# Cached keys turned by VectorE, and sample weights regrouped by one product, in a fused decoder step

## What is computed

```python
def dilated_attention_sample(q, k_all, v_all, rel_bias):
    # q: (B,T,H,Dh) are the last T rows of k_all/v_all: (B,L,H,Dh)
    for (w, d) in ((128, 1), (512, 4), (2048, 16)):
        n_k = w // d
        dist = d * jnp.arange(n_k + 1)
        idxs.append(q_idx[:, None] - dist[None, :]); biases.append(pattern_bias(rel_bias, d, n_k))
    ...
    s = einsum('bthc,btkhc->bthk', q, kg) * HEAD_DIM ** -0.5 + bias
    p = softmax(s)
    return einsum('bthk,btkhc->bthc', p, vg)
```

## Time and profile before

| | us |
|---|---|
| median of 3 runs (1082.96 to 1085.27) | 1083.66 |
| the profiled execution, its own time | 1082.67 |
| its span, first to last instruction | 1080.7 |
| PE busy / DVE / ACT / POOL | 1036.0 / 523.0 / 312.7 / 212.4 |
| convolution stage, 280 to 498 us | 218 |

### The profile page before, as it was taken

One profiled execution on the slowest core, in us unless ns is written; L12 is line 12 of the kernel. 1 busy time (PEld: TensorE's weight loads), 2 busy tenths in 40 slices (PEclk: granted clock), 3 DMA queues, 4 the chain that ended last, 5 costly groups with the idle time before them and its releaser, 6 DMA issues.

```text
span 1080.7 us, 15684 instructions
## 1 busy us (share of the span) xinstructions
PE 1036.0 (96%) x5834; PEld 620.1 (57%) x5834; DVE 523.0 (48%) x1175; ACT 312.7 (29%) x665; POOL 212.4 (20%) x240
## 2 busy tenths in 40 slices
PE   7999999999999999999999999989999999889997
PEld 6888875565878777766555554334433333345443
DVE  6836634777733464545556464441111110047674
ACT  2332313777533322301111123111111111244331
POOL 0100001121433352531012111322231110130000
PEclk9999999999999999999999998989999999989999
DMA  9713214940563666663973237989999999974321
GB/s 315 190 31 116 71 50 119 293 101 6 215 213 112 212 211 216 207 244 81 355 270 128 94 105 280 405 340 414 418 410 410 419 420 399 371 288 157 119 78 78
DMA packets 99260, 242.11 MB, mean 224 GB/s; under 512 B 21206, under 2 KB 56958, under 8 KB 84528
## 3 DMA queue, kind: packets, MB, share of 16 engines
q1 hardware_dynamic: 88544, 212.10, 54.1%
q0 software_dynamic: 9920, 26.38, 6.4%
q10 hardware_dynamic: 720, 2.62, 0.6%
HBM read 210.12 MB, written 35.65 MB: 227 GB/s over the span
## 4 chain that ended last, share of the span: by engine, by line
PE 80%; DVE 6%; DMA 6%; SPq 4%; issue 2%; ACT 2%; POOL 0%; POOLq 0%; DVEq 0%; ACTq 0%
PE pair L2921 13%; PE pair L3124 13%; PE pair L2598 10%; PE pair L2976 9%; PE pair L3146 6%; PE pair L3228 5%; PE pair L3223 3%; PE pair L2739 2%; DMA h_dram<-R 2%; DMA R<-in_w_up 2%; PE pair L2713 2%; PE pair L3047 2%; PE pair L2755 2%; PE pair L3111 1%; SPq L707 1%
## 5 line engine op out<-in xcount | busy, mean ns | idle before, releaser
L2921 PE MATMUL pair<-R 128*128 128x264 f32 x672 | 160.2, 389 | 0.2 <-POOL R L1032 0.2
L3124 PE MATMUL pair<-R 128*32 128x512 f32 (+2 forms) x896 | 151.3, 601 | 5.2 <-DMA R<-in_w_up 3.0
L2598 PE MATMUL pair<-R 128*128 128x256 f32 x672 | 149.7, 382 | 0.4 <-DVE R L1755 0.4
L2598 PEld LDWEIGHTS pair<-R 128*128 128x128 f32 x672 | 127.0, 191 | 18.8 <-issue 1.0
L2921 PEld LDWEIGHTS pair<-R 128*128 128x128 f32 x672 | 123.5, 190 | 23.4 <-issue 3.5
L2976 PE MATMUL pair<-R 128*128 128x512 f32 x256 | 116.6, 606 | 0.0
L2329 DVE TENSOR_TENSOR R<-pair,R 128x256 f32<-128x256 f32 x21 | 8.9, 425 | 208.3 <-ACT R L1516 208.3
L3124 PEld LDWEIGHTS pair<-R 128*32 128x32 f32 (+2 forms) x896 | 48.8, 125 | 92.2 <-issue 87.8
L3146 PE MATMUL pair<-R,bias 128*32 128x512 f32 (+2 forms) x448 | 78.0, 611 | 2.7 <-issue 2.1
L2976 PEld LDWEIGHTS pair<-R 128*128 128x128 f32 x256 | 47.7, 192 | 53.3 <-issue 52.6
L3228 PE MATMUL pair<-R 128*128 128x512 f32 x168 | 73.0, 593 | 0.0
(11 more groups left out here) (366 smaller groups left out, 1471.5 us busy)
## 6 DMA issues: line engine op xcount, KB each, us to landing
R<-in_w_gate SPq DMA_DIRECT2D x32, 1024.0 KB, 12.3
R<-in_w_up SPq DMA_DIRECT2D x32, 1024.0 KB, 15.6
R<-in_w_down SPq DMA_DIRECT2D x32, 1024.0 KB, 16.8
R<-in_w_in SPq DMA_DIRECT2D x12, 1024.0 KB, 8.4
R<-in_x_prompt SPq DMA_DIRECT2D x16, 512.0 KB, 3.8
R<-in_cache_k SPq DMA_DIRECT2D x8, 1024.0 KB, 5.0
R<-in_cache_v SPq DMA_DIRECT2D x8, 1024.0 KB, 4.9
R<-y_dram SPq DMA_DIRECT2D x16, 512.0 KB, 5.9
```

The costliest lines, as they stand in the source:

```text
L2598: last = mm(qbank(p, part, k), lhs[:, c, :], rhs[:, c, :], start=(c == 0), stop=(c == 3))
L2921: last = mm(cbank(n, k), lhs[:, c, :], rhs[:, c, :], start=(c == 0), stop=(c == 3))
L3124: last = mm(bk[2 + u][r, :].rearrange("p (w f) -> p w f", w=2), xgT[u][:, c, r], wgu[s][:, :, c, :], start=(c == 0), stop=(c == DC - 1))
```

## The change

Keys are no longer transposed by PE. DVE turns 32x32 blocks of them straight from the ring slot into `kT` (two instructions per part), so each of the sixteen 32-dimension slices of the heads (n = 4j + 2hh + half) has its keys in quarters: partition strip i holds quarter i of the rows. A score is 16 matmuls of 256 columns against a `qbd` in which q is spread over the strips with zeros elsewhere. The softmax goes over two sequences at a time (4 passes in place of 2); since a query's scores now lie in four partitions, minima and sums are combined by small DVE transposes (`by_group`). The weights are moved into place by one product with a permutation matrix (`turn`) and one DVE transpose (`put`). The cache items come in another order, and a key's ring slot is free when DVE has turned it. The `relbd` loads are a quarter as large and come behind two stores of x in SP's queue; the sample's q and k are turned by 32 small matmuls; 16 copies (`q4`) lie in steps 9 to 24 of the prompt attention.

```diff
-ITEMS = [("k", b) for b in range(5)] + [("v", 0), ("k", 5), ("v", 1), ("k", 6), ("v", 2), ("k", 7)] + [("v", b) for b in range(3, NB)]
+ITEMS = [("k", 0), ("k", 1), ("k", 2), ("v", 0), ("k", 3), ("v", 1), ("k", 4), ("v", 2),
+         ("k", 5), ("v", 3), ("k", 6), ("v", 4), ("k", 7), ("v", 5), ("v", 6), ("v", 7)]
...
+def sample_order():
+    parts = []
+    for g in range(NPASS + 1):
+        keys = [[("key", 2 * g + d, gg) for gg in range(NG)] if g < NPASS else [] for d in range(2)]
+        if g == 0:
+            parts += keys[0] + [("score", 0)] + keys[1] + [("score", 1), ("soft", 0)]
+            continue
+        b = 2 * g - 2
+        parts += [*keys[0][0:2], ("norm", g - 1), *keys[0][2:3], ("turn", g - 1), *keys[0][3:4], ("put", g - 1)]
+        if g < NPASS:
+            parts += [("score", 2 * g)]
+        parts += [("weigh", b), *keys[1][0:2], ("sum", b), ("weigh", b + 1), *keys[1][2:4]]
+        if g < NPASS:
+            parts += [("score", 2 * g + 1), ("soft", g)]
+        parts += [("sum", b + 1)]
+    return parts
-ROOM = {"key": 4, "score": 4, "turn": 6, "weigh": 8, "sum": 4}
+ROOM = {"key": 4, "score": 6, "soft": 2, "norm": 2, "turn": 2, "put": 2, "weigh": 8, "sum": 4}
...
@@ SP: relbd, now behind keep_xT(0) and keep_xT(1); the ring
+        for t in range(NT):
+            for hh in range(2):
+                const(relbd[NBUCKET * t:NBUCKET * t + NBUCKET, 16 * hh + t:P:32], I["rel_bias"][:, hh:H:2])
-                    sp.wait_ge(S("kn_full"), 4 * ub + 4)
-                    sp.wait_ge(S("kf_full"), 4 * ub + 4)
+                    sp.wait_ge(S("kt_done"), 4 * ub + 4)
@@ ACT: keep_near, keep_far and keep_ps are gone
+            for s in range(2):
+                act.activation(Es[:, s, :], Es[:, s, :], ACT.Exp, bias=nms[:, s:s + 1], scale=-1.0, accum_out=dens[:, s:s + 1]).then_inc(S("ss_exp"), 1)
@@ DVE, prompt attention
+            if 9 <= n < 25:
+                i, j = divmod(n - 9, 4)
+                dve.tensor_copy(q4[32 * i:32 * i + 32, 4 * j:4 * j + 4, :], qts[32 * j:32 * j + 32, :, :]).then_inc(S("qbd"), 1)
@@ DVE, convolution stage
+        def spread_q(b):
+            dve.tensor_tensor(qbd[b % 2][:, :, 16:32].rearrange("p n (i t) -> p n i t", i=4),
+                              q4[:, :, NT * b:NT * b + NT].unsqueeze(2).broadcast_to([P, 16, 4, NT]),
+                              in_strip.unsqueeze(1).unsqueeze(3).broadcast_to([P, 16, 4, NT]), ALU.mult).then_inc(S("qbd"), 1)
+        def turn_keys(b, gg):
...
+                if b >= 1:
+                    dve.wait_ge(S("ss_done"), b)
...
+            dve.transpose(out[:, 0:4], raw[:, 0:4])
+            dve.transpose(out[:, 4:7], raw[:, 4:7]).then_inc(S("kt_done"), 1)
+        def by_group(cols, op, src, group, out):
+            then(dve.transpose(cols, src))
+            then(dve.tensor_reduce(group, cols.rearrange("p (h i t) -> p h t i", h=2, i=4), AX.X, op))
+            if op == ALU.add:
+                then(dve.reciprocal(group, group))
+            return dve.transpose(out.rearrange("p (h i t) -> p h i t", h=2, i=4),
+                                 group.rearrange("p (h t) -> p h t", h=2).unsqueeze(2).broadcast_to([P, 2, 4, NT]))
...
+            for s in range(2):
+                then(dve.tensor_tensor_reduce(Es[:, s, :], bk[6 + g % 2][:, ROW * s:ROW * s + ROW], bias_s, -1.0, 3e38, ALU.add, ALU.min,
+                                              least[:, s:s + 1]))
+                if 2 * g + s + 1 < NB:
+                    new_bias(2 * g + s + 1)
+            by_group(least_t, ALU.min, least, group_least, nms).then_inc(S("ss_scored"), 1)
...
+        def put_ps(g):
+            dve.wait_ge(S("st_full"), g + 1)
+            if g >= 1:
+                dve.wait_ge(S("so_full"), 2 * g)
+            dve.transpose(PTs.rearrange("p s c x -> p (s c x)"), bk[4]).then_inc(S("st_done"), 1)
@@ PE
+            pe.wait_ge(S("kt_done"), NG * b + NG)
...
+            for hh in range(2):
+                for half in range(2):
+                    for j in range(NG):
+                        n = 4 * j + 2 * hh + half
+                        at = 32 * n + (0 if hh else 16)
+                        last = mm(out[strips[j], ROW * second:ROW * second + ROW], qbd_all[second][:, at:at + 32], kT[:, n, :],
+                                  start=(second == 0 and hh == 0 and half == 0), stop=(second == 1 and hh == 1 and half == 1))
         def turn_ps(g):
+            pe.wait_ge(S("ps_ready"), 2 * g + 2)
...
+            mm(bk[4], regroup, Es.rearrange("p s n -> p (s n)"), start=True, stop=True).then_inc(S("st_full"), 1)
```

More of the change, by code:

```diff
@@ L112, in constants @@
[L112 to L117, removed]
-    r = np.arange(P)
-    c["c_mask"] = (2 * (r[:, None] % 32 // 8) + r[:, None] % 2 == np.arange(AD)[None, :] // DH).astype(np.float32)
-    c["c_sel"] = (r[:, None] % 8 // 2 == np.arange(NT)[None, :]).astype(np.float32)
+    c["c_hot_s"] = hot.reshape(P, SKN).astype(np.float32)
@@ new lines, in constants @@
+    r = np.arange(P)
+    quarter, token = r % 16 // NT, r % NT
+    log = np.full((P, PART + SAMP + NB * SAMP), NEG, np.float32)
+    for i in range(4):
+        log[quarter == i, 0:PART] = log_count(dist[i])[token[quarter == i]]
+    for b in range(NB):
+        own = (np.arange(SAMP)[None, :] // NT == b) & (quarter[:, None] == 0)
+        log[:, PART + SAMP + SAMP * b:PART + 2 * SAMP + SAMP * b] = np.where(own, log_count(new_dist)[token], NEG)
+    c["c_log_s"] = log
+    row_at = 32 * quarter + 8 * (r // 32) + 4 * (r % 32 // 16) + token
@@ L197 @@
[L197 to L206, removed]
@@ L224, with place_of @@
 PARTS_AT = spread_parts()
-def place_of(kind, b, gg=None):
-    return next(s for s, parts in PARTS_AT.items() for part in parts if part[0:2] == (kind, b) and (gg is None or part[2] == gg))
+def place_of(part):
+    return next(s for s, parts in PARTS_AT.items() if part in parts)
 NSTAT = 6
@@ L2096, in sample_part @@
         def sample_part(kind, b, *more):
-            if "norm" in more:
-                normalise_sample(0 if kind == "key" else 1)
+            if kind == "key":
+                turn_keys(b, more[0])
+            if kind == "soft":
+                score_sample(b)
+            if kind == "norm":
+                normalise_sample(b)
+            if kind == "put":
+                put_ps(b)
             if kind == "weigh":
                 mask_sample(b)
-            if "soft" in more:
-                score_sample(b // 4)
-            if kind == "score" and b == 3:
-                spread_q(1)
-                new_bias(1)
             if kind == "sum":
                 keep_sum(b)
-            if "sum" in more:
-                keep_sum(more[-1])
         dve.wait_ge(S("late_in"), 16 * NLATE)
@@ L2867, in weigh_values @@
             for k in range(FARC):
[L2868 to L2869 removed]
+                mm(bk[3][strips[k], :], PTs[:, second, 4 + k, :], KV[slot][:, 4 + k, :], start=False, stop=True)
+            last = mm(bk[3][strips[3], :], PTs[:, second, 7, :], V[:, PT, :], start=False, stop=True)
             last.then_inc(S("so_full"), 1)
@@ L2888, in sample_part @@
         def sample_part(kind, *more):
-            if kind == "key":
-                keys(more[0], more[1])
             if kind == "score":
```

292 lines of the change are left out of this document (127 added, 165 removed).

## The result

The changed kernel takes 1092.95 us in the median of 8 runs (1089.7 to 1098.08), the kernel before 1083.06 us in 8 runs beside it (1080.61 to 1085.88). The ratio is 1.0093 with a 95% interval of 1.0074 to 1.0112: **slower by 9.9 us**, where 4.4 us less was forecast and the range ended at 1089.

What follows compares the result with a forecast made beforehand. PE's busy time was taken to bound the convolution stage. PE work -22.3, new waits for DVE +16.9, head -0.8 and prompt attention +1.8 gave -4.4 us: 1078.3 by the sum, 1079.3 predicted as median, range 1069 to 1089.

Steps and rivals of the forecast that it cites:

- PE's own work: Convolution stage: key parts and weight turns leave PE, scores and permutation products add some; 22.3 us less for PE.
- DVE's prices: Convolution stage: a key part's two transposes cost DVE about 1.2 us; DVE busy about 165 us in all.
- rival with stretched transposes: Convolution stage: beside GpSimd a key part takes DVE 1.75 us, making DVE the bound; 1088 to 1097 us, chance 0.20.
- low end's price: Range's low end, 1069 us: DVE keeps up, with a key part's transposes at 0.8 us, as the weights' scaling runs.
- (a): Stage start: scores 0 and 1 wait for cleared regions, spreads, new keys and eight key parts on DVE; 3.5 us.
- (b): Pass 0, from score 1 in slot 13 to the turn behind slot 19: PE waits 3.6 us for DVE.
- (c): Pass 1, score 4 behind put, while DVE also loads transposed convolution terms: PE waits 2.2 us.
- (d): Pass 2, at the turn and score 6: PE waits 2.1 us for DVE.
- (e): Pass 3: norm and turn share a slot, put and weigh 6 another; PE waits 3.0 and 2.6, together 5.6 us.
- The prompt attention: Prompt attention: 32 small matmuls add 1.1 us, the q4 copies on DVE 0.7; together +1.8 us.
- rival of late weights: Convolution stage: weight loads arrive late in some six groups, so 5 us come back; 1084 us, chance 0.13.
- "slower" rival: Slower outcome, chance 0.22: mainly DVE becoming the bound through stretched transposes (1088 to 1097 us), a little late weights.

Runs made afterwards that it cites:

- gaps filled: Changed kernel with extra PE products, their results overwritten, in four places where PE only waited for DVE; 1087.74 us, ratio 1.0056 to before.
- norm first: Changed kernel with the norm ahead of the next sequence's keys in DVE's list, turns unmoved; 1091.03 us, ratio 1.0083 to before.
- and tail: As norm first, with pass 3's norm, turn, put and first weighing in slots of their own, earlier parts moved up; 1081.31 us, ratio 0.9983 to before.
- less DVE work: Changed kernel without turning each key part's three far pieces from the second sequence on; whole run 2205.99 us, only the 216.6 us stage is read.
- head's loads moved: Changed kernel with the small relbd loads back in their old place, ahead of the two stores of x; 1090.54 us, ratio 1.0070 to before.
- q4 on GpSimd: Changed kernel with the 16 small q4 copies of the prompt attention done by GpSimd, not DVE; 1090.36 us, ratio 1.0060 to before.
- ScalarE's help: As and tail, with ScalarE taking the weights' division and q's spreading for sequences 2 to 7 from DVE; 1076.62 us, ratio 0.9943 to before.
- all of it: As ScalarE's help, plus q4 copies on GpSimd, ScalarE's spreading moved to turn and put, new keys' copies on ScalarE; 1075.23 us, ratio 0.9913 to before.
- before, with gaps: Kernel before the change with only four added PE waits on chained ScalarE instructions in the convolution stage; 1098.93 us, ratio 1.0129 to before.

## Why the prediction was wrong

The whole stage in the ledger, all in us:

| run | length | PE's waits | time at 1.2 GHz | left: work |
|---|---|---|---|---|
| before | 218.2 | 1.1 | 0 | 217.1 |
| after | 227.8 | 20.9 | 20.5 | 196.7 |
| gaps filled | 221.5 | 12.6 | 3.4 | 207.2 |
| norm first | 225.5 | 20.9 | 17.0 | 196.1 |
| and tail | 215.9 | 15.7 | 6.8 | 196.8 |
| less DVE work | 216.6 | 16.5 | 6.8 | 196.7 |
| head's loads moved | 226.2 | 21.3 | 17.1 | 196.4 |
| q4 on GpSimd | 225.6 | 20.2 | 17.1 | 196.8 |
| ScalarE's help | 209.2 | 12.6 | 0 | 196.6 |
| all of it | 209.1 | 10.9 | 3.4 | 196.5 |
| before, with gaps | 232.9 | 10.2 | 10.3 | 217.5 |

The last column is worked out from the others, with half of the low clock. It agrees within 0.7 us over the eight kernels with PE's same work (all but before, gaps filled, and before with gaps), while their low clock runs from 0 to 20.5 us. So the three terms account for the stage to that size.

- **PE's own work: right.** 22.3 us less were forecast, 1.1 of them waits, so 21.2 of work; measured 20.4. One price in it was off: a product among products takes 1.85 us (in the chain of before three in a row take 5.54 at 449.52), not the 1.78 it takes between transposes, so a key part cost PE 0.68 to 0.7:

```profile
449.52 5.54 PE pair L2921 x24
```

  With 0.69 the sum would have been 19.0. The new scores took 1.87 us from their start to the next piece, for 1.88 in the sum. Of the 1.4 that remain 0.7 may be the low clock inside a wait; the rest I didn't split. The 16 in the last line of the earlier trace rows are records, so eight matmuls; the 0.86 each is right.
- **DVE's prices: right.** 1.23 us per key part for 1.2; DVE 157 us busy for 165. The rival with stretched transposes is out by the two rows of the transposes. Its premise is right for the joins with both operands in R, 0.81 beside a working GpSimd for 0.43. The low end's price was taken from the weights' scaling; that scaling runs so fast only while GpSimd idles, 0.61 us for two of 256 elements, and takes 1.26 to 1.50 beside GpSimd.
- **The waits: right place by place, low by 4.0 us.** Against the ledger of the prediction: (a) 4.2 for 3.5 (1.8 at a product, 1.06 and 1.30 at scores 0 and 1), (b) 3.9 for 3.6, (c) 2.9 for 2.2 (0.58 at the turn and 2.31 at score 4), (d) 2.0 for 2.1, (e) 5.8 for 5.6, the rest 2.1 for 1.7. The sum of 18.7 would have been low by 2.2; the 1.8 that I took off for overlapping starts wasn't there.
- **The step that failed: "what the clock does" was missing.** The prediction read in the earlier trace rows that the clock stood at 2.4 GHz nearly throughout and carried that over to a kernel in which PE waits at the turns for 2 to 4 us at a time. Behind three of these places and two more waits (score 4, the first weighing of pass 3) it ran at 1.2 GHz, 20.5 us in all, 10.2 us of cost. The earlier trace rows counts gaps of up to 1.6 us in the prompt attention, and the trace of before has 3.4 us of low clock there, behind two of 1.9 and 1.6 us:

```profile
192.00:194.00 2.00, 1.59 (x8) 1.52 (x8) 1.96 (x8) 0.86 (x4) 0.00 (x0) 0.62 0.93 173
194.00:196.00 2.00, 2.00 (x22) 0.73 (x20) 1.95 (x4) 1.66 (x5) 0.00 (x0) 0.53 1.00 211
```

  That is what could have warned.
- **The prompt attention: +2.3 for +1.8, split wrongly.** The 32 small matmuls take 0.68 us from their start to PE's next piece, for the 0.61 of the earlier trace rows, so 0.1 in place of 1.1. The q4 copies cost 0.7 to 2.0 for 0.7, inside the ends of 0 and 3.3; PE waits there for DVE. What else of the 2.3 there is, is open.
- **The head: 0.8 forecast, about 0.6** as a mean over the profiles, within what single ones move.
- **Weights late, and the rest:** waits for GpSimd 0.8 us in two places; the rival of late weights is out. What lies behind the stage took 580.8 us for 582.4.

Together: -5.4 forecast for the stage, +9.6 measured; the 15.0 between are 10.2 of clock, 4.0 of waits and 0.8 of work. Without the clock's term the kernel would have come out about level with before; without the other two misses it would still have been slower, by some 5 us. The "slower" rival had the time nearly right (1088 to 1097) for a reason that wasn't there.

## What to carry to other kernels

When a change turns a PE that is always busy into one that waits in a few places, give its longer waits a second term, taken from a stretch of low clock behind such a gap in any profile at hand (here 1.7 us each, behind gaps of 2.5 to 3.1 us), and look for places where two parts of a chain stand in adjoining slots. Before counting on a lighter PE, check whether the engine that takes the work has it in the right order and at the right time: a slot or two more between norm, turn, put and weigh, and earlier places for the parts ahead of them, were worth 9.7 us here, and the same change with it and with an idle ScalarE's help beats the kernel before by 0.9%. A gap that can't be removed can be filled: 12 products whose result is thrown away made this kernel faster.

## What the hardware showed that I had not expected

- Filling PE's gaps with useless products shortened the stage by 6.3 us, though they are 10.3 us of work.
- A gap of 2.80 us and one of 2.27 had no low clock behind them, one of 2.50 and one of 2.48 had; of two gaps of 2.01 at the same place of two kernels, one had.
- A division of the weights, two instructions of 128x256, took 0.61 us while GpSimd idled and 1.26 to 1.50 while it worked.
- 32 matmuls of 32x32 (64 records) take 0.68 us up to PE's next piece, eight transposes of the same data 0.61.
